# Small and large experts in turn, and part of the weight lows on GpSimd, in a two-block transformer kernel on one core

## The chip, the cores and the metric

The kernel runs on one NeuronCore of a Trainium2 chip. The time is device microseconds of one execution of the whole program. Lower is better.

## The reference

Two blocks are computed for 256 tokens of width 1024, everything in float32. The first has three attention branches and a SwiGLU feed-forward layer. The second has an HGRN2 layer with a feed-forward layer, then differential attention, and at the end a mixture of experts. Only the last part is touched by the change:

```
def moe_swiglu(h, w_router, w_gate, w_up, w_down):        # 256 tokens, D = 1024
    logits = (hf @ w_router).astype(jnp.float32)           # 8 experts
    top_val, top_idx = lax.top_k(logits, TOP_K)            # TOP_K = 2
    gates = jax.nn.softmax(top_val, axis=-1)
    ...
    return (jax.nn.silu(xb @ w_gate[e]) * (xb @ w_up[e])) @ w_down[e]   # D_FF_EXPERT = 3584
```

Each token goes to two of eight experts. An expert has three weight matrices of 1024 x 3584 (gate, up) and 3584 x 1024 (down), 44 MB in float32, and 352 MB are read for all eight.

## The kernel before

**Arithmetic.** A float32 product is made of three passes on TensorE in its faster float32 form: high part times high part, high times low and low times high (`mm3`, L425 to L427). So each weight has to be split. ScalarE makes the high part (`hi`, L1179) by a copy that rounds, and VectorE makes the low part, `lo = src - hi` (L1748), with both inputs in SBUF.

**Pieces.** The weights come through a ring of 2 MB slots, three and in the expert part four, by DMAs that SyncE issues in the order of the list `WL`. In the expert part one slot is two pieces of 128 x 2048. Each piece has one place out of four (`WHB0`, `WHB1`, `WHX0`, `WHX1` for the high parts, `WLB`/`WLX` for the low). ScalarE may make piece n only when TensorE has used piece n - 4 (`s_used`), VectorE when ScalarE has made the high part (`s_hi`), TensorE when VectorE has made the low (`s_lo`), and SyncE loads into a slot again when both its pieces have their low parts. An expert is 21 slots, so 42 pieces: 7 chunks of 512 hidden columns with 2 pieces each of gate, up and down. All eight make 336 pieces, in a list that is fixed when the program is built.

**Large and small experts.** Experts are taken in an order that the chip works out from the number of tokens of each (`order`, L2352 and on): `RANK[i]` says the expert of which rank is taken at turn i. Turn 0 is always expert 0, which the program counts as rank 0, and the others follow by size. Turns in `LIGHT` have room for 64 tokens, the others for 128. In a large turn TensorE makes three passes for each weight tile. In a small one the high and low part of 64 tokens stand side by side as one 128-column stationary operand, so that two passes do (L1007, L1008 for gate and up, L1053, L1054 for down): a piece is 12 matmuls of 512 columns in a large turn and 8 in a small one. A small turn also adds its halves up when the hidden values are turned (L1031) and has two short VectorE operations a chunk for it (L2412 and L2416), where a large turn has two longer ones (L2419 and L2426). Before, turns 1, 4 and 7 are small, and five are large. If an expert has more tokens than its turn has room for, a second pass over all experts (`pe_second` and its like) follows. It compares a count that the chip works out with a limit, and was not run in the execution shown.

**Order on the engines.** Each engine's program is written by hand. TensorE goes through the pieces one by one, gathers the next expert's tokens inside the last step of an expert (`gather`, L984 in small turns, L986 in large ones, the second half at the same place of each turn) and adds the one before to the result in between. ScalarE and VectorE have the pieces between the other work: ScalarE runs ahead of TensorE by up to four pieces in program order and VectorE by up to three (`split_to`). GpSimd has nothing to do in the expert part after the start but the roots of the last norm (L2574) and a quarter of its rows (L2596, L2598).

Of the kernel before, what the change touches and what calls it, by code (L numbers as in the profile page):

```python
# [8 lines left out]
F32 = mybir.dt.float32  # L9
# [3 lines left out]
ALU = mybir.AluOpType  # L13
# [7 lines left out]
NE = 8  # L21
# [7 lines left out]
LIM = 128  # L29
LIM_L = 64  # L30


RANK = (0, 5, 1, 2, 6, 3, 4, 7)
LIGHT = (1, 4, 7)


def steps_of(ex):
# [84 lines left out]
def build(nc, I, table, out):  # L122
    ctx = ExitStack()
    with ctx:
# [62 lines left out]
        def sem(name):  # L187
            return ctx.enter_context(nc.semaphore(name))
# [1 line left out]
        s_ring = [sem(f"s_ring{i}") for i in range(NSLOT + 1)]  # L190
        s_full = [sem(f"s_full{i}") for i in range(8)]
        s_out = [sem(f"s_out{i}") for i in range(8)]
        s_hi, s_lo, s_used = sem("s_hi"), sem("s_lo"), sem("s_used")
        s_colh, s_cols = sem("s_colh"), sem("s_cols")
        s_ms, s_rs, s_z, s_za = sem("s_ms"), sem("s_rs"), sem("s_z"), sem("s_za")
        s_ssq, s_ss1, s_sq = sem("s_ssq"), sem("s_ss1"), sem("s_sq")
# [84 lines left out]
        BEFORE = [max((j for j in range(i) if SLOT[j] == SLOT[i]), default=-1) for i in range(len(WL))]  # L281
# [3 lines left out]
        PIECES, PLACE, AFTER, LAST_OF = [], [], [], []  # L285
        FIRST = {}
        lay = {}
        for part_name, part_list, n_p in (("A", WL_A, 4), ("F1", WL_F1, 2), ("C", WL_C, 4), ("F2", WL_F2, 2), ("E", WL_E, 4), ("M", WL_M, 2)):
            FIRST[part_name] = len(PIECES)
            for item in part_list:  # L290
                step = -(-item[3] // n_p)
                for j in range(n_p):
                    k = len(PIECES)
# [11 lines left out]
                    PLACE.append(place)  # L305
                LAST_OF.append(len(PIECES) - 1)
        NP = len(PIECES)
        HIS, LOS = WHB + WHX, WLB + WLX

        def piece(k):  # L310

            i, t0, t1 = PIECES[k]
            n = WL[i][4]
            m = (t1 - t0) * n
            b, at = PLACE[k]
            return slot(i)[:, t0 * n:t1 * n], HIS[b][:, at:at + m], LOS[b][:, at:at + m]
# [90 lines left out]
        def pe_program(e):  # L407
            pe = Stream(e, s_pe)
# [6 lines left out]
            def next_piece(name, key):  # L415
                k = at[0]
                at[0] += 1
                i, t0, t1 = PIECES[k]
                assert WL[i][:2] == (name, key), (WL[i][:2], name, key)
                pe.wait_ge(s_lo, k + 1)  # L420
                _, hi, lo = piece(k)
                return hi.rearrange("p (t n) -> p t n", t=t1 - t0), lo.rearrange("p (t n) -> p t n", t=t1 - t0), (s_used, k + 1)

# [434 lines left out]
            for tt in range(2):  # L858
                for g in range(2):
# [9 lines left out]
                    for j in range(4):  # L869
# [3 lines left out]
                        if tt == 0:  # L873
                            t = e.matmul(o, STT[:, 0, h, :], v0, start=True, stop=True)
                        else:
                            e.matmul(o, STT[:, 2, h, :], v0, start=True, stop=False)
                            t = e.matmul(o, STT[:, 1, h, :], v1, start=False, stop=True)
# [859 lines left out]
        def dve_program(e):  # L1737
            v = Stream(e, s_dve)
            at = [0]

            def split_to(k):

                while at[0] <= min(k, NP - 1):
                    n = at[0]
                    at[0] += 1
                    src, hi, lo = piece(n)
                    v.wait_ge(s_hi, n + 1)
                    e.tensor_tensor(lo, src, hi.bitcast(F32), ALU.subtract).then_inc(s_lo, 1)  # L1748

            done = [0]  # L1750
# [198 lines left out]
            for i, w in enumerate((WFG, WRT)):  # L1949
                t = v.step(e.tensor_copy(W8[2 * i][:, :, :], w[:, :, :]))  # L1950
# [143 lines left out]
            t = v.step(e.tensor_tensor(LBM, L3[:, 0, :], L3[:, 1, :], ALU.max))  # L2094
            v.wait_ge(*t)
            t = v.step(e.tensor_tensor(LBM, LBM, L3[:, 2, :], ALU.max))
# [71 lines left out]
            for n in ("hg0", "hg1", "hv0", "hv1"):  # L2168
                for q in range(4):
# [3 lines left out]
                    if (n, q) in LEVEL_AT:  # L2173
                        i = LEVEL_AT[n, q]
# [177 lines left out]
            def order():  # L2352

                v.wait_ge(s_one, 2)
                t = v.step(e.memset(NCNT[:, 0:1], 999.0))
                v.wait_ge(*t)
                oth = NCNT.unsqueeze(1).to_broadcast([128, 8, 8])
                own = NCNT.unsqueeze(2).to_broadcast([128, 8, 8])
                v.step(e.tensor_tensor(C4[:, 0], oth, own, ALU.is_gt))
                t = v.step(e.tensor_tensor(C4[:, 1], oth, own, ALU.is_equal))  # L2360
                v.wait_ge(*t)
                t = v.step(e.tensor_tensor(C4[:, 1], C4[:, 1], tri, ALU.mult))
                v.wait_ge(*t)
                t = v.step(e.tensor_tensor(C4[:, 0], C4[:, 0], C4[:, 1], ALU.add))
                v.wait_ge(*t)
                t = v.step(e.tensor_reduce(RNK, C4[:, 0], AX.X, ALU.add))
                v.wait_ge(*t)
                t = v.step(e.tensor_scalar(CAPV, RNK, 4.5, float(LIM - LIM_L), ALU.is_lt, ALU.mult))
                eight = CT[:, C_IOTA:C_IOTA + 8]
                t2 = v.step(e.tensor_tensor(C4[:, 0], RNK.unsqueeze(1).to_broadcast([128, 8, 8]), eight.unsqueeze(2).to_broadcast([128, 8, 8]), ALU.is_equal))  # L2370
                v.wait_ge(*t)
                t = v.step(e.tensor_scalar(CAPV, CAPV, float(LIM_L), None, ALU.add))
                v.wait_ge(*t2)
                t2 = v.step(e.tensor_tensor(C4[:, 1], C4[:, 0], eight.unsqueeze(1).to_broadcast([128, 8, 8]), ALU.mult))
                v.wait_ge(*t2)
                t2 = v.step(e.tensor_reduce(MX8[:, 0, :], C4[:, 1], AX.X, ALU.add))
                v.wait_ge(*t2)
                e.tensor_copy(EID[:, :], MX8[0:1, 0, :]).then_inc(s_perm, 1)
                v.wait_ge(*t)
                v.wait_ge(s_rte, 2)  # L2380
                for src, dst in ((POS, POSR), (G, GR)):
                    if src is G:
                        v.wait_ge(s_gw, 2)
                    for tt in range(2):
                        t = v.step(e.tensor_tensor(Q4[:, tt], C4[:, 0], src[:, tt, :].unsqueeze(1).to_broadcast([128, 8, 8]), ALU.mult))
                    v.wait_ge(*t)
                    for tt in range(2):
                        t = e.tensor_reduce(dst[:, tt, :], Q4[:, tt], AX.X, ALU.add)
                    if src is G:
                        t.then_inc(s_gw, 1)  # L2390
                    else:
                        v.wait_ge(*v.step(t))
                t = v.step(e.tensor_tensor(MX8[:, 1, :], CNT0, CAPV, ALU.subtract))
                v.wait_ge(*t)
                t = v.step(e.tensor_reduce(MOST, MX8[:, 1, :], AX.X, ALU.max))
                v.wait_ge(*t)
                e.tensor_scalar(CNT[:, :], MOST[0:1, :], float(LIM), None, ALU.add).then_inc(s_most, 1)
# [171 lines left out]
        def pool_program(e):  # L2569
# [30 lines left out]
            def norm_vectors(k):  # L2600
                for j, name in enumerate(("ln_g_2", "ln_b_2")):
                    e.dma_start(BC[:, j, :], spread(I[name][k * D:k * D + D], D)).then_inc(s_ln, 16)
# [104 lines left out]
            p.wait_ge(s_hp, 11)  # L2707
            p.wait_ge(s_hd, 1)
            norm_vectors(3)
            for tt in range(2):  # L2710
                inverse_root(("ln3", tt))
            gain_rows(3, 1, 1)
# [4 lines left out]
        def sp_program(e):  # L2717
            q = Stream(e, s_pe)

            def source(i):  # L2720
                if WL[i][2] is not None:
                    return WL[i][2]
                kind, ex = WL[i][0].split()
                ex, at_ = int(ex), WL[i][1]
                w = I[f"moe_w_{kind}_2"]
                if ex and (kind, at_) == ("gate", (0, 0)):
                    q.wait_ge(s_perm, 1)
                    T["expert", ex] = e.value_load(EID[0:1, RANK[ex]:RANK[ex] + 1], min_val=0, max_val=NE - 1)
                w = w[bass.ds(T["expert", ex], 1)] if ex else w[0:1]
                if kind == "down":  # L2730
                    return w.rearrange("o (a p b) n -> p (o a) (b n)", p=128, b=2)[:, at_ // 2:at_ // 2 + 2, :]
                c0, k0 = at_
                return w.rearrange("o (t p) n -> p (o t) n", p=128)[:, k0:k0 + WL[i][3], c0:c0 + WL[i][4]]

            def load(i):
                t, n = WL[i][3:]
                if BEFORE[i] >= 0:
                    q.wait_ge(s_lo, LAST_OF[BEFORE[i]] + 1)
                elif SLOT[i] == NSLOT:
                    q.wait_ge(s_used, FIRST["E"])  # L2740
                    e.dma_start(CT2[:, :], table[:, C_LAST:C_END]).then_inc(s_tab2, 16)
                src = source(i)
                e.dma_start(slot(i)[:, 0:t * n].rearrange("p (t n) -> p t n", t=src.shape[1]), src).then_inc(s_ring[SLOT[i]], 16)

            load(0)
            e.dma_start(H[:, :, :], I["x"].rearrange("(a p) n -> p a n", p=128)).then_inc(s_x, 16)
            load(1)
            load(2)
            e.dma_start(LEVS, table[:, C_KEEP:C_LAST]).then_inc(s_lvt, 16)
            for i in range(NSLOT, len(WL)):  # L2750
                load(i)
            q.wait_ge(s_most, 1)
            q.wait_ge(s_lo, NP)
            n_most = e.value_load(CNT[0:1, 0:1], min_val=0, max_val=S + LIM)
            with e.If(n_most > LIM):
                sp_second(e)
            q.wait_ge(s_outd, 32)
# [148 lines left out]
```

## Time and profile before

| | us |
|---|---|
| runs (median, lowest, highest) | 2044.85, 2043.73, 2046.56 |
| profiled execution, its own time | 2045.65 |
| profiled execution, span of the trace | 2043.9 |

| engine | busy us | share |
|---|---|---|
| PE (TensorE matmul) | 1922.6 | 94% |
| DVE (VectorE) | 1507.5 | 74% |
| ACT (ScalarE) | 1211.3 | 59% |
| POOL (GpSimd) | 158.2 | 8% |

The span is that of the profiler from the first to the last instruction. The expert part takes the last half: its first piece is split at 1049.8 us and its last at 2007.6 us. In all rows "<-" in a name stands between what is written and what is read, and "<-" behind a wait stands ahead of what ended it. The rows further down are copied from the page and from views of the same trace.

### The profile page before, as it was taken

Reading aid. Unit: us, or ns where it says so; the run is one execution under the profiler, and the core shown is the slowest. Engines: PE = TensorE matmul, PEld = TensorE weight load, DVE = VectorE, ACT = ScalarE, POOL = GpSimd, SP = SyncE. Lnnn points to the kernel's source line nnn. Section 1 sums busy time; section 2 is a strip of 40 time slices with the busy share of each in tenths; the row PEclk is TensorE's granted clock in tenths of the full one; section 3 lists DMA queues with packets and bytes.
Section 4 is the critical chain, followed back from the end, with each engine's and each line's share of the span. In section 5 each row is a group of like instructions: output and inputs, shape, how many; then the busy total and the mean of one; then the engine's idle time right before and its main releaser. Section 6 shows DMA issues by size and latency. Waiting matters only on the chain.

```text
span 2043.9 us, 22687 instructions
## 1 busy us (share of the span) xinstructions
PE 1922.6 (94%) x9319; PEld 1583.1 (77%) x9319; DVE 1507.5 (74%) x1433; ACT 1211.3 (59%) x1229; POOL 158.2 (8%) x123
## 2 busy tenths in 40 slices
PE   5999999999998899989779999999999999999994
PEld 4778777888987688867557887888888788888873
DVE  4645456544689754476568889998988999898996
ACT  4554445433553444344336778876778887777883
POOL 1401010000133300031120000000000000000000
PEclk9999999999999899989778999999999999999997
DMA  8433334554432455344146999999999999999991
GB/s 275 150 136 127 124 124 166 205 185 169 161 124 83 168 205 203 127 162 165 42 169 231 376 359 404 409 397 352 351 364 366 411 408 387 351 359 363 373 409 75
DMA packets 154318, 511.64 MB, mean 250 GB/s; under 512 B 4334, under 2 KB 8672, under 8 KB 139872
## 3 DMA queue, kind: packets, MB, share of 16 engines
q1 hardware_dynamic: 151888, 502.91, 65.6%
q0 software_dynamic: 1424, 4.59, 0.8%
q10 hardware_dynamic: 896, 2.62, 0.3%
q8 instruction: 76, 1.25, 0.2%
q14 instruction: 34, 0.28, 0.0%
HBM read 509.05 MB, written 1.05 MB: 250 GB/s over the span
## 4 chain that ended last, share of the span: by engine, by line
PE 75%; DVE 14%; DMA 4%; ACT 3%; issue 2%; POOL 1%; DVEq 0%; SPq 0%; ACTq 0%; POOLq 0%
PE PS L425 21%; PE PS L427 21%; PE PS L426 21%; DVE WLB L1748 4%; DVE WLX L1748 4%; DMA ring<-in_moe_w_down 3%; PE PS L986 1%; PE PS L1053 1%; PE PS L1054 1%; DMA ring<-in_w_mem_kv 1%; PE PS L928 1%; PE PS L558 1%; ACT WHB L1179 1%; PE PS L1035 1%; DVE AR L2135 1%
## 5 line engine op out<-in xcount | busy, mean ns | idle before, releaser
L1748 DVE TENSOR_TENSOR WLB<-ring,WHB 128x2048 fp32r<-128x2048 f32 (+1 forms) x344 | 647.0, 1898 | 134.2 <-ACT WHB L1179 133.7
L1179 ACT ACTIVATE WHB<-ring 128x2048 fp32r<-128x2048 f32 (+1 forms) x344 | 534.5, 1562 | 347.7 <-PE PS L427 327.2
L1748 DVE TENSOR_TENSOR WLX<-ring,WHX 128x2048 fp32r<-128x2048 f32 (+1 forms) x216 | 468.4, 2190 | 56.7 <-ACT WHX L1179 56.5
L1179 ACT ACTIVATE WHX<-ring 128x2048 fp32r<-128x2048 f32 (+1 forms) x216 | 394.8, 1839 | 176.8 <-PE PS L427 156.8
L425 PE MATMUL PS<-WHB,XH 128*128 128x512 f32 (+1 forms) x640 | 258.9, 405 | 11.0 <-DVE XL L1799 6.8
L427 PE MATMUL PS<-WHB,XL 128*128 128x512 f32 (+1 forms) x640 | 252.0, 394 | 0.0
L426 PE MATMUL PS<-WLB,XH 128*128 128x512 f32 (+1 forms) x640 | 251.2, 393 | 0.0
L425 PEld LDWEIGHTS PS<-WHB,XH 128*128 128x128 f32 x640 | 123.5, 193 | 37.4 <-issue 11.5
L2574 POOL TENSOR_TENSOR SM<-SM,MH 128x8 f32<-128x8 f32 (+3 forms) x28 | 36.8, 1319 | 1468.7 <-DVE SM L1761 1468.7
L427 PEld LDWEIGHTS PS<-WHB,XL 128*128 128x128 f32 x640 | 122.9, 192 | 26.4
L426 PEld LDWEIGHTS PS<-WLB,XH 128*128 128x128 f32 x640 | 123.4, 193 | 23.9
L425 PE MATMUL PS<-WHB,EH 128*128 128x512 f32 x280 | 111.1, 397 | 0.0
L425 PE MATMUL PS<-WHX,EH 128*128 128x512 f32 x280 | 110.9, 396 | 0.0
L427 PE MATMUL PS<-WHB,EL 128*128 128x512 f32 x280 | 109.7, 392 | 0.0
L427 PE MATMUL PS<-WHX,EL 128*128 128x512 f32 x280 | 109.4, 391 | 0.0
L426 PE MATMUL PS<-WLB,EH 128*128 128x512 f32 x280 | 109.4, 391 | 0.0
L426 PE MATMUL PS<-WLX,EH 128*128 128x512 f32 x280 | 109.0, 389 | 0.0
L425 PE MATMUL PS<-WHX,XH 128*128 128x512 f32 (+1 forms) x240 | 92.0, 383 | 4.7 <-DVE WLX L1748 4.7
L425 PE MATMUL PS<-WHB,HTH 128*128 128x512 f32 x240 | 94.3, 393 | 0.0
L427 PE MATMUL PS<-WHB,HTL 128*128 128x512 f32 x240 | 93.5, 390 | 0.0
L426 PE MATMUL PS<-WLB,HTH 128*128 128x512 f32 x240 | 93.4, 389 | 0.0
L427 PE MATMUL PS<-WHX,XL 128*128 128x512 f32 (+1 forms) x240 | 91.1, 379 | 0.0
(398 smaller groups left out, 3472.6 us busy)
## 6 DMA issues: line engine op xcount, KB each, us to landing
ring<-in_moe_w_gate SPq DMA_DIRECT2D x56, 2048.0 KB, 9.9
ring<-in_moe_w_up SPq DMA_DIRECT2D x56, 2048.0 KB, 10.3
ring<-in_moe_w_down SPq DMA_DIRECT2D x56, 2048.0 KB, 10.3
ring<-in_w_in SPq DMA_DIRECT2D x13, 2048.0 KB, 8.1
ring<-in_hg_w_in SPq DMA_DIRECT2D x8, 2048.0 KB, 8.5
ring<-in_da_w_in SPq DMA_DIRECT2D x6, 2048.0 KB, 8.0
ring<-in_w_gate SPq DMA_DIRECT2D x5, 2048.0 KB, 8.6
ring<-in_w_up SPq DMA_DIRECT2D x5, 2048.0 KB, 7.8
```

Of the source, the lines that this page charges most:

```text
L425: e.matmul(o, xh, wh, start=start, stop=False)
L426: e.matmul(o, xh, wl, start=False, stop=False)
L427: return e.matmul(o, xl, wh, start=False, stop=stop)
L558: e.matmul(PS[2][:, a0:a1], q_[o:o + 64, j, 128 * qt:128 * qt + 128], k_[o:o + 64, j, 0:n], start=True, stop=False)
L928: e.matmul(PS[b][:, a0:a1], QD[o:o + 64, h, 128 * qt:128 * qt + 128], KD[o:o + 64, h, 0:n], start=True, stop=False)
L986: t = e.matmul(PS[b][:, 128 * j:128 * j + CAP], src[:, tt, 128 * d:128 * d + 128], PO[:, tt, :], start=(tt == 0), stop=(tt == 1))
L1035: t = e.transpose(PS[6][:, 128 * j:128 * j + 128], inner(HID[:, i, :], j), ident)
L1053: e.matmul(PS[4 + q][:, :], HTH[:, i, xs], hi[:, jj, cs], start=first, stop=False)
L1054: t = e.matmul(PS[4 + q][:, :], HTH[:, i, xs], lo[:, jj, cs], start=False, stop=end)
L1179: e.activation(hi, src, ACT.Copy).then_inc(s_hi, 1)
L1748: e.tensor_tensor(lo, src, hi.bitcast(F32), ALU.subtract).then_inc(s_lo, 1)
L2574: e.tensor_tensor(RR[name], RV[name], MH[:, 0:RR[name].shape[1]], ALU.pow).then_inc(s_rs, 1)
```

## The change

There are two edits. First, `RANK` and `LIGHT` make four turns large and four small, in turn: 0, 2, 4 and 6 are large and 1, 3, 5 and 7 small. The limit between large and small ranks follows (4.5 becomes 3.5). Second, from the ninth piece of the expert part on (`SHARED`), VectorE makes only the first 1536 of a piece's 2048 columns of the low part, and GpSimd makes the other 512, with the same operation and its own semaphore `s_lp`, for which TensorE and SyncE now also wait. GpSimd's 328 new instructions stand in its program between the loads of the last norm's vectors and the roots of that norm.

```
-RANK = (0, 5, 1, 2, 6, 3, 4, 7)
-LIGHT = (1, 4, 7)
+RANK = (0, 4, 1, 5, 2, 6, 3, 7)
+LIGHT = (1, 3, 5, 7)
+HEAVY = NE - len(LIGHT)
...
+        SHARED = FIRST["M"] + 8
+        OWN = 1536
...
                 pe.wait_ge(s_lo, k + 1)
+                if k >= SHARED:
+                    pe.wait_ge(s_lp, k - SHARED + 1)
...
                     src, hi, lo = piece(n)
                     v.wait_ge(s_hi, n + 1)
+                    if n >= SHARED:
+                        src, hi, lo = src[:, 0:OWN], hi[:, 0:OWN], lo[:, 0:OWN]
                     e.tensor_tensor(lo, src, hi.bitcast(F32), ALU.subtract).then_inc(s_lo, 1)
...
-                t = v.step(e.tensor_scalar(CAPV, RNK, 4.5, float(LIM - LIM_L), ALU.is_lt, ALU.mult))
+                t = v.step(e.tensor_scalar(CAPV, RNK, HEAVY - 0.5, float(LIM - LIM_L), ALU.is_lt, ALU.mult))
...
             norm_vectors(3)
+            for n in range(SHARED, NP):
+                src, hi, lo = piece(n)
+                p.wait_ge(s_hi, n + 1)
+                e.tensor_tensor(lo[:, OWN:], src[:, OWN:], hi[:, OWN:].bitcast(F32), ALU.subtract).then_inc(s_lp, 1)
             for tt in range(2):
                 inverse_root(("ln3", tt))
...
                 if BEFORE[i] >= 0:
                     q.wait_ge(s_lo, LAST_OF[BEFORE[i]] + 1)
+                    if LAST_OF[BEFORE[i]] >= SHARED:
+                        q.wait_ge(s_lp, LAST_OF[BEFORE[i]] - SHARED + 1)
...
             q.wait_ge(s_lo, NP)
+            q.wait_ge(s_lp, NP - SHARED)
```

TensorE at the start of turn 3, whose first gate piece lies in the place `WHX0`/`WLX0`; `EH` and `EL` are the high and low parts of the gathered tokens, `HID` the hidden values of the chunk before. Before, and then of the changed kernel:

```order
L427 MATMUL PS<-WHB1,HTL 128x512
L425 MATMUL PS<-WHX0,EH 128x512
L426 MATMUL PS<-WLX0,EH 128x512
L427 MATMUL PS<-WHX0,EL 128x512
L425 MATMUL PS<-WHX0,EH 128x512
L426 MATMUL PS<-WLX0,EH 128x512
L427 MATMUL PS<-WHX0,EL 128x512
L425 MATMUL PS<-WHX0,EH 128x512
```

```order
L433 MATMUL PS<-WHB1,HTL 128x512
L1013 MATMUL PS<-WHX0,EH 128x512
L1014 MATMUL PS<-WLX0,EH 128x512
L1013 MATMUL PS<-WHX0,EH 128x512
L1014 MATMUL PS<-WLX0,EH 128x512
L1013 MATMUL PS<-WHX0,EH 128x512
L1014 MATMUL PS<-WLX0,EH 128x512
L1013 MATMUL PS<-WHX0,EH 128x512
L1014 MATMUL PS<-WLX0,EH 128x512
```

The third pass of each weight tile is gone in this turn (the line numbers are higher by 6 to 16 through the edits themselves). Turns 4 to 7 change their kind as the new tables say.

VectorE in the second step of turn 3, before and then changed; L1748 is the low part of a piece (L1756 after the change), L2448 (L2456) adds a part of the expert before to the result:

```order
L1748 TENSOR_TENSOR WLB<-ring,WHB 128x2048
L1748 TENSOR_TENSOR WLX<-ring,WHX 128x2048 x2
L2426 TENSOR_TENSOR HID<-PS,HID 128x512 x2
L1748 TENSOR_TENSOR WLB<-ring,WHB 128x2048
L2448 TENSOR_TENSOR H<-H,PS 128x512
L1748 TENSOR_TENSOR WLB<-ring,WHB 128x2048
L1748 TENSOR_TENSOR WLX<-ring,WHX 128x2048 x2
L2419 TENSOR_TENSOR HTL<-PS,HTH 128x512
```

```order
L1756 TENSOR_TENSOR WLB<-ring,WHB 128x1536
L1756 TENSOR_TENSOR WLX<-ring,WHX 128x1536 x2
L2420 TENSOR_TENSOR SGT<-PS,SGT 128x256
L1756 TENSOR_TENSOR WLB<-ring,WHB 128x1536
L2424 TENSOR_TENSOR HTH<-SGT,HTH 128x4x64
L1756 TENSOR_TENSOR WLB<-ring,WHB 128x1536
L1756 TENSOR_TENSOR WLX<-ring,WHX 128x1536
L2456 TENSOR_TENSOR H<-H,PS 128x512
```

The pieces keep their places in the row and are shorter; the two operations on 512 columns of a large turn give way to two on 256.

GpSimd at the end of its program, before and then changed; the two DMAs are the vectors of the last norm, L2574 (later L2582) its roots:

```order
L2706 MEMSET HID 128x128
L2602 DMA BC<-in_ln_g_2 128x1024
L2602 DMA BC<-in_ln_b_2 128x1024
L2574 TENSOR_TENSOR SM<-SM,MH 128x1 x2
L2596 TENSOR_TENSOR H<-LZ,BC 128x512
L2598 TENSOR_TENSOR H<-H,BC 128x512
```

```order
L2714 MEMSET HID 128x128
L2610 DMA BC<-in_ln_g_2 128x1024
L2610 DMA BC<-in_ln_b_2 128x1024
L2721 TENSOR_TENSOR WLB0<-ring,WHB0 128x512
L2721 TENSOR_TENSOR WLB1<-ring,WHB1 128x512
L2721 TENSOR_TENSOR WLX0<-ring,WHX0 128x512
L2721 TENSOR_TENSOR WLX1<-ring,WHX1 128x512
```

The 328 new instructions follow one another, each behind the wait for its high part, and nothing else of GpSimd's stands between them.

## Rows read from the trace of the kernel before

**Rows 1.** The page, part 1: busy us, share of the span, instructions.
```profile
PE 1922.6 (94%) x9319; PEld 1583.1 (77%) x9319; DVE 1507.5 (74%) x1433; ACT 1211.3 (59%) x1229; POOL 158.2 (8%) x123
```

**Rows 2.** Busy time by stretch: PE, PEld, DVE, ACT, POOL, then PEclk, DMA share, GB/s.
```profile
1190.00:1297.00 107.00, 103.67 (x508) 84.06 (x506) 102.15 (x65) 90.53 (x72) 0.00 (x0) 1.00 0.99 386
...
1417.00:1541.00 124.00, 124.00 (x579) 103.55 (x578) 108.17 (x67) 89.44 (x61) 0.00 (x0) 1.00 0.94 355
1541.00:1648.00 107.00, 104.03 (x512) 84.66 (x511) 102.63 (x65) 91.19 (x73) 0.00 (x0) 1.00 0.99 389
```

**Rows 3.** Chain of waits, longest parts: start us, us; second gathers, ahead of turns 1 to 7.
```profile
1190.94 1.71 PE PS L984 x16
...
1296.30 1.74 PE PS L986 x16
...
1417.77 1.74 PE PS L986 x16
...
1541.94 1.71 PE PS L984 x16
...
1646.79 1.74 PE PS L986 x16
...
1768.26 1.74 PE PS L986 x16
...
1892.43 1.71 PE PS L984 x16
```

**Rows 4.** Instructions in order of time, PE: the last matmul on weights.
```profile
2017.70 0.39 PE L1054 MATMUL PS<-WLX,HTH 128*128 128x512 f32 x1
```

**Rows 5.** Waits in 1190 to 1297 us (a small turn): total us, times, longest.
```profile
PEld PS L1007 <- DVE WLB L1748: 2.9, 5, 1.1
...
DVE WLB L1748 <- ACT WHB L1179: 2.7, 2, 2.3
```

**Rows 6.** Waits in 1417 to 1541 us (a large turn).
```profile
ACT WHB L1179 <- PE PS L427: 18.1, 20, 2.2
```

**Rows 7.** Instructions in order of time, DVE, small turn: start us, us for all, count.
```profile
1233.62 4.49 DVE L1748 TENSOR_TENSOR WLX<-ring,WHX 128x2048 fp32r<-128x2048 f32 x2
```

**Rows 8.** The same view near the start, pieces of half the size.
```profile
79.91 2.36 DVE L1748 TENSOR_TENSOR WLB<-ring,WHB 128x1024 fp32r<-128x1024 f32 x2
...
85.71 1.21 DVE L1748 TENSOR_TENSOR WLB<-ring,WHB 128x1024 fp32r<-128x1024 f32 x1
```

**Rows 9.** The same view, POOL, while DVE has nothing under way.
```profile
704.48 1.30 POOL L2598 TENSOR_TENSOR H<-H,BC 128x512 f32<-128x512 f32 x1
```

**Rows 10.** The same view, POOL and DVE from 603 to 611 us.
```profile
604.29 4.47 POOL L2664 TENSOR_TENSOR BC<-BC,NG 128x512 f32<-128x512 f32 x2
```
```profile
602.25 3.18 DVE L2135 TENSOR_TENSOR AR<-AR 128x1024 f32<-128x1024 f32 x1
605.35 4.50 DVE L1748 TENSOR_TENSOR WLB<-ring,WHB 128x1024 fp32r<-128x1024 f32 x2
```

**Rows 11.** The same view, DVE: one instruction beside POOL's, and without.
```profile
896.92 1.25 DVE L2047 SCALAR_TENSOR_TENSOR SM<-SM 128x1 f32<-128x1 f32 x1
```
```profile
1047.53 0.16 DVE L2047 SCALAR_TENSOR_TENSOR SM<-SM 128x1 f32<-128x1 f32 x1 [0.66 <-POOL SM L2574]
```

**Rows 12.** The same view, POOL and DVE from 260.7 to 261.8 us.
```profile
260.70 1.28 POOL L2635 TENSOR_TENSOR AR<-AR 128x512 f32<-128x512 f32 x1 [65.03 <-DVE AR L1897]
```
```profile
260.54 1.89 DVE L1897 TENSOR_TENSOR AR<-PS,AR 128x512 f32<-128x512 f32 x3
```

**Rows 13.** DVE by groups, 1190 to 1297 us, then 1417 to 1541 us: busy us, mean ns.
```profile
L1748 DVE TENSOR_TENSOR WLX<-ring,WHX 128x2048 fp32r<-128x2048 f32 x22 | 49.9, 2285 | 1.2 <-ACT WHX L1179 1.2
...
L2416 DVE TENSOR_TENSOR HTH<-SGT,HTH 128x256 fp32r<-128x256 f32 x5 | 2.1, 418 | 0.0
```
```profile
L2419 DVE TENSOR_TENSOR HTL<-PS,HTH 128x512 fp32r<-128x512 f32 x7 | 4.8, 689 | 5.5 <-ACT HTH L1638 5.5
```

**Rows 14.** Busy time by stretch, 20 us inside a small turn.
```profile
1620.00:1640.00 20.00, 19.91 (x106) 16.68 (x104) 19.78 (x16) 17.43 (x15) 0.00 (x0) 1.00 1.02 413
```

More of the change, by code:

```diff
@@ L192, in build @@
         s_out = [sem(f"s_out{i}") for i in range(8)]
-        s_hi, s_lo, s_used = sem("s_hi"), sem("s_lo"), sem("s_used")
+        s_hi, s_lo, s_lp, s_used = sem("s_hi"), sem("s_lo"), sem("s_lp"), sem("s_used")
         s_colh, s_cols = sem("s_colh"), sem("s_cols")
```

## The prediction

> **What bounds the kernel now.** I read the page first: TensorE is busy for 94% of the span and VectorE for 74%, GpSimd for 8% [rows 1]. That share is a mean over stages, so the second view is busy time by stretch, one stretch for each expert turn. A large turn (1417 to 1541 us) has TensorE busy for all of its 124 us and VectorE for 108.17. A small one (1190 to 1297) has VectorE at 102.15 of 107 and the DMA engines at 0.99 [rows 2]. Third come the waits. In the small turn TensorE's weight loads wait for VectorE's low parts, and VectorE waits only 2.7 us for ScalarE [rows 5]; in the large one ScalarE waits for TensorE to free a place [rows 6]. So large turns are TensorE's, and small turns VectorE's, with the DMA close behind.
>
> The length of a turn is best read on TensorE, from the second gather of one turn to that of the next, 42 pieces apart [rows 3]: small turns take 1296.30 - 1190.94 = 105.4 and 1646.79 - 1541.94 = 104.9 us; a large turn behind a small one 1417.77 - 1296.30 = 121.5 and again 121.5; a large one behind a large one 124.2 and again 124.2. Behind the last gather come 48 pieces (six of turn 6, and turn 7), which end with the last matmul on weights at 2018.1 [rows 4]: 125.7 us, which is 48/42 of 105.2 and 5.5 for the drain. From 1190.94 to 2018.1 are 827.2 us. Before the first gather there are 36 pieces of turn 0, which is large in both kernels.
>
> **Edit one, the order of the turns.** The kinds from turn 1 on were S L L S L L S and become S L S L S L S. One large turn becomes small, and each large one then stands behind a small one. By the rows: 3 x (105.2 + 121.5) + 125.7 = 805.8 us, 21.4 less. A small turn does not go below its 105 even if VectorE is helped: an expert is 168 instructions less on TensorE but the same 44.04 MB (21 slots of 2.097 MB), and at the 413 GB/s of the busiest rows [rows 14] these take 106.6 us. So the DMA is what is late next, and the first edit alone, or both if GpSimd cost nothing, is worth about -21 us.
>
> **Edit two, who makes the low part.** VectorE's piece: two of 2048 columns in a row take 4.49 us, one 2.285 [rows 7, 13], so each further one adds 2.21. Of 1024 columns it is 2.36 for two and 1.21 for one [rows 8], so 1.15. For 1536 I take the middle, 1.68. GpSimd's 512 columns take 1.30 us alone [rows 9], well under the 2.5 to 3.0 that a piece lasts in a turn, so it would be hidden if the two engines ran side by side.
>
> They don't. At 604 us GpSimd had two operations of just this size (512 columns, both inputs in SBUF) while VectorE made two low parts of 1024 columns: GpSimd's two took 4.47 us and not 2.6, VectorE's two 4.50 and not 2.36 [rows 10]. GpSimd's first could not run before VectorE's L2135 ended at 605.43; from there to 609.85, the end of VectorE's second, both had two to do, and 4.42 us is the sum of both. The engines took turns, each waiting for the whole of the other's instruction. Per pair it is 4.47 / 2 = 2.23 us, of which 1.15 are VectorE's, so 512 columns of GpSimd's hold VectorE up for 1.08. Even an operation on one column waits so: 1.25 us beside GpSimd's, 0.16 without [rows 11]. Where VectorE reads one operand from PSUM, neither is slowed: three of 512 columns in 1.89 us and GpSimd's at 1.28 [rows 12].
>
> The Trainium skill says why, in "SBUF — State Buffer", section "Who interferes with whom": a VectorE instruction with two SBUF inputs gets its second one through the read interface that it shares with GpSimd, and it and a GpSimd instruction that reads SBUF exclude each other for a whole instruction. By that rule this change moves work from an engine to a port that the same engine needs; by the plain reading of the GpSimd row alone it would be free.
>
> So the two engines together need 1.68 + 1.08 = 2.76 us a piece, where VectorE alone needed 2.21. The sum over the engines' timelines:
>
> - A small turn: 42 x 2.76 = 115.9. L2416 also has both inputs in SBUF: seven of 0.42, less the overlap of 0.07 between neighbours, are 2.4. The other VectorE work of a small turn reads PSUM (L2412, L2448, ZL, POT). What a turn has besides pieces is 105.2 - 42 x 2.21 = 12.4 us. Most of it can lie beside GpSimd's piece, since GpSimd's turn comes behind each VectorE piece and a short PSUM operation fits into 1.08. I leave 1.2 exposed, one in six of the operations. That is 119.5 us against 105.2.
> - A large turn: TensorE needs 124.2 in the steady state and 121.5 behind a small one. VectorE now needs 115.9 and its 14 operations L2419 and L2426 of 0.69, the combines, and waits for ScalarE of 5.5 us before L2419 [rows 13]; hidden in the same way they leave some 5. So VectorE needs about 121 of what TensorE needs 121.5. I take 121.5, no change, but the slack of 124 - 108 that let VectorE get ahead for the next small turn is gone.
> - Before the first gather: 36 pieces of a large turn, 28 of them shared, at 2.76 less than TensorE's own 124.2 / 42 = 2.96. I take +1.
> - The last 48 pieces: 119.5 x 48 / 42 + 5.5 = 142.1, against 125.7.
>
> Together 1 + 3 x (119.5 + 121.5) + 142.1 = 866.1, against 827.2: +38.9 us, made of -21.4 from the order and +60 from the taking of turns. The rest costs nothing: TensorE's and SyncE's second waits are for an engine that isn't behind VectorE, because GpSimd's row is not held up by other work; a slot is then freed with VectorE's part as now, and the loads, at 0.94 to 0.99 of the DMA's time before [rows 2], get more time. Behind GpSimd's 328 instructions stand only the roots of the last norm, which wait for the end anyway. On the profiled time of 2045.65 that gives 2084.5; its distance to the median of the runs (-0.8) leaves 2083.7.
>
> The bounds of what the trace doesn't show, the overlap: if nothing but pieces and L2416 is exposed, a small and a large turn take 2 x 115.9 + 2.4 = 234.2 together (TensorE can be late in the large one and catch up in the small), the end 118.3 x 48 / 42 + 5.5 = 140.7, and the sum is 1 + 702.6 + 140.7 - 827.2 = +17. If nothing is hidden, a small turn is 115.9 + 12.4 = 128.3, a large one 115.9 + 15 = 131, the end 152: 2 + 778 + 152 - 827 = +105. With no exclusion at all it is -21. I am nearer to the lower end since the alternation in [rows 10] leaves the 1.08 us slot behind every piece.
>
> **Rivals.**
> 1. The two engines do not exclude each other here, or hardly: faster. It would hold if GpSimd fell into VectorE's PSUM operations and idle time always, or if the lock hung on the operands used at 604 us. Place: small turns. Price: 2045.65 - 21.4 - 0.8, 2023 us. For it: in a small turn VectorE has 12.4 us of such time and GpSimd is free to run ahead of it. Against it: GpSimd needs 42 x 1.08 = 45 us, nearly four times that. The point from which it decides: the order gives 21.4 us, the small turns and the end have 174 pieces, so a piece in them may cost 2.51 + 0.12 = 2.63 us with all around it, and the pieces alone take 2.76 by [rows 8 to 10]. The Trainium skill has a table in "SBUF — State Buffer", section "A bandwidth-pool intuition that's wrong (but worth ruling out)", that gives HBM about 358 GB/s a core; by it a small turn would need 123 us, and no order of turns could gain. The measured 413 decides here.
> 2. Excluded, but all else hidden: the +17 above, 2062 us, and down to 2050 if GpSimd holds VectorE up for 1.04 us and not 1.08 (328 x 0.04 = 13). For it: GpSimd has no other work to be queued behind. Against it: ScalarE can be only four pieces ahead of TensorE, so GpSimd often has nothing to do just when VectorE turns to a PSUM operation.
> 3. Excluded, and the engines' hand-offs get in each other's way: VectorE's late L2419 holds TensorE up in large turns too, since the slack that hid it is gone. Up to +105, 2150 us. For it: four places are little room.
> 4. The change doesn't do what it says, because the fifth expert in size has over 64 tokens and the second pass runs. The routing worked out from the reference on its inputs gives 127, 28, 62, 85, 35, 37, 41 and 97 tokens. Expert 0 is large anyway, then 97, 85 and 62; the first small one has 41. So it doesn't run. It would read 352 MB again, at 413 GB/s 853 us more.
>
> **How the numbers follow.** My forecast, 2062 to 2112 us, has 0.70; rival 1 0.10, rival 2 0.11, rival 3 (2112 to 2150) 0.08, rival 4 0.01. The range of 8 in 10 is 2052 to 2112: it leaves out rival 1 and the top. What a measurement of this kernel can tell from no change is 0.2%, 4 us. Faster by more: rival 1 and a little, 0.11. Within it: 0.04, from the lower end of rival 2. Slower: 0.85.
>
> **What would show it.** In the profile after, GpSimd's pieces should last 2 to 2.8 us and not 1.3 where VectorE is at work, and VectorE's 1536-column pieces up to 2.8, not 1.75, so that VectorE's busy time in the expert part grows although it has a quarter less to do. Small turns should be 117 to 123 us apart and large ones 120 to 125. TensorE should wait for VectorE's low parts in small turns for over 10 us. It is wrong if VectorE's pieces have a mean under 1.9 us or small turns stay near 105. The granted clock should stay at 1.00 in the turns; if it falls in the small ones, where TensorE now idles more, they last longer than said.

## The result and the profile after

The changed kernel takes 2080.1 us (median of 4 runs, 2078.24 to 2082.75); the kernel before, on the same chip, 2044.62. The ratio is 1.0173, 95% interval 1.0156 to 1.0191: slower by 35.5 us. The forecast was 2084, in a range from 2052 to 2112. The profiled execution has a span of 2080.9 us.

The second gathers of the turns in the chain of waits (start us, us), which answer to [rows 3]:

```profile
1192.22 1.71 PE PS L990 x16
...
1433.32 1.71 PE PS L990 x16
...
1553.12 1.74 PE PS L992 x16
...
1674.63 1.71 PE PS L990 x16
...
1795.54 1.73 PE PS L992 x16
...
1917.07 1.71 PE PS L990 x16
```

The one missing in this view, ahead of turn 2, starts at 1310.23 in the order of time, where all the others start 0.16 us earlier than here, so it counts as 1310.4. So the small turns 1, 3 and 5 take 118.2, 119.8 and 120.9 us (before: 105.4 and 104.9), the large turns 2, 4 and 6 take 122.9, 121.5 and 121.5. The last matmul on weights ends at 2055.1, 138.0 us after the last gather, against 125.7.

Busy time by stretch, for turns 1 to 4, with the columns of [rows 2]:

```profile
1192.00:1310.00 118.00, 105.85 (x494) 83.00 (x494) 112.95 (x63) 90.74 (x71) 103.76 (x42) 0.99 0.96 360
1310.00:1433.00 123.00, 122.17 (x580) 101.88 (x579) 119.91 (x73) 90.25 (x64) 90.28 (x43) 1.00 0.99 373
1433.00:1553.00 120.00, 107.47 (x497) 84.20 (x496) 114.96 (x65) 91.15 (x71) 101.05 (x42) 0.97 0.96 360
1553.00:1674.50 121.50, 121.50 (x580) 101.95 (x579) 116.62 (x71) 90.00 (x64) 94.72 (x43) 1.00 0.98 372
```

VectorE (third pair) has a quarter less to subtract and is busy for 113 to 120 us a turn instead of 102 to 108. GpSimd is busy for 90 to 104 us with work that needs 42 x 1.3 = 55 alone. The DMA engines move 360 GB/s in the small turns instead of 386 to 389, at a share of 0.96 and not 0.99. They are not the limit there any more: in turn 1 the chain of waits has no load in it, VectorE's pieces are 78% of it, and none of ScalarE's waits there is for a load.

The groups of the two engines from 1110 to 1950 us (busy us, mean ns, idle before), to be held against [rows 13] and [rows 9]:

```profile
L1756 DVE TENSOR_TENSOR WLB<-ring,WHB 128x1536 fp32r<-128x1536 f32 x146 | 359.5, 2476 | 15.9 <-ACT WHB L1185 15.5
...
L2721 POOL TENSOR_TENSOR WLX<-ring,WHX 128x512 fp32r<-128x512 f32 x146 | 353.2, 2429 | 76.7 <-ACT WHX L1185 76.4
...
L2424 DVE TENSOR_TENSOR HTH<-SGT,HTH 128x256 fp32r<-128x256 f32 x21 | 21.0, 999 | 4.4 <-ACT HTH L1641 4.4
```

A VectorE piece of 1536 columns lasts 2.48 us on average, more than one of 2048 did (2.285). In order of time, inside turn 1, first VectorE and then GpSimd:

```profile
1229.55 1.51 DVE L2424 TENSOR_TENSOR HTH<-SGT,HTH 128x256 fp32r<-128x256 f32 x1
1230.97 2.84 DVE L1756 TENSOR_TENSOR WLX<-ring,WHX 128x1536 fp32r<-128x1536 f32 x1
1233.73 2.83 DVE L1756 TENSOR_TENSOR WLB<-ring,WHB 128x1536 fp32r<-128x1536 f32 x1
1236.49 0.68 DVE L2456 TENSOR_TENSOR H<-H,PS 128x512 f32<-128x512 f32 x1
1237.09 2.23 DVE L1756 TENSOR_TENSOR WLB<-ring,WHB 128x1536 fp32r<-128x1536 f32 x1
```
```profile
1227.97 2.80 POOL L2721 TENSOR_TENSOR WLX<-ring,WHX 128x512 fp32r<-128x512 f32 x1
1230.73 4.22 POOL L2721 TENSOR_TENSOR WLB<-ring,WHB 128x512 fp32r<-128x512 f32 x2
1234.91 2.79 POOL L2721 TENSOR_TENSOR WLX<-ring,WHX 128x512 fp32r<-128x512 f32 x1
```

The two steps from 1230.97 to 1233.73 to 1236.49 are 2.76 us each, the sum that the prediction had: 1.68 of VectorE's and 1.08 of GpSimd's. At 1236.49 VectorE turns to an operation that reads PSUM; it is not lengthened (0.68), GpSimd's turn lies beside it, and the piece behind it has only 2.23 instead of 2.84. That is the hiding that the sum counted on. The 256-column L2424, with both inputs in SBUF, has 1.51 instead of 0.42.

Who waits in turn 1 (total us, times, longest), for [rows 5]:

```profile
PEld PS L1013 <- DVE WLX L1756: 9.0, 7, 2.5
...
PEld PS L1013 <- DVE WLB L1756: 4.9, 7, 1.1
```

TensorE's weight loads wait 13.9 us for VectorE in these two rows. They hardly wait for GpSimd's part; in the groups from 1110 to 1950 us:

```profile
L1013 PE MATMUL PS<-WHX,EH 128*128 128x512 f32 x184 | 76.4, 415 | 16.9 <-DVE WLX L1756 16.2 <-POOL WLX L2721 0.7
L1013 PE MATMUL PS<-WHB,EH 128*128 128x512 f32 x184 | 76.0, 413 | 9.1 <-DVE WLB L1756 7.5 <-POOL WLB L2721 1.3
```

### The profile page after: what moved, and what is told of

Its sections match the earlier page's. It is cut to its first block, busy times and chain, and to the rows that moved or that the text cites. A ratio compares the mean times of both kernels' runs of the same rounds, so it can differ in the third digit from the quotient of the medians.

```text
span 2080.9 us, 23288 instructions
## 1 busy us (share of the span) xinstructions
PE 1915.5 (92%) x9235; PEld 1564.0 (75%) x9235; DVE 1581.4 (76%) x1431; ACT 1216.3 (58%) x1243; POOL 934.0 (45%) x451
## 4 chain that ended last, share of the span: by engine, by line
PE 65%; DVE 28%; issue 3%; ACT 3%; DMA 1%; POOL 1%; DVEq 0%; ACTq 0%; POOLq 0%
PE PS L431 18%; PE PS L433 18%; PE PS L432 18%; DVE WLB L1756 10%; DVE WLX L1756 10%; PE PS L1059 1%; PE PS L1060 1%; DVE HTH L2424 1%; PE PS L934 1%; DMA ring<-in_w_mem_kv 1%; PE PS L564 1%; DVE AR L2143 1%; PE PS L992 1%; PE PS L845 1%; PE PS L990 1%
## 5 line engine op out<-in xcount | busy, mean ns | idle before, releaser
L1756 DVE TENSOR_TENSOR WLB<-ring,WHB 128x1536 fp32r<-128x1536 f32 (+2 forms) x344 | 680.0, 1992 | 134.1 <-ACT WHB L1185 133.6
L1756 DVE TENSOR_TENSOR WLX<-ring,WHX 128x1536 fp32r<-128x1536 f32 (+2 forms) x216 | 495.5, 2317 | 54.6 <-ACT WHX L1185 54.5
L2721 POOL TENSOR_TENSOR WLX<-ring,WHX 128x512 fp32r<-128x512 f32 x164 | 401.0, 2455 | 85.4 <-ACT WHX L1185 85.0
L2721 POOL TENSOR_TENSOR WLB<-ring,WHB 128x512 fp32r<-128x512 f32 x164 | 379.5, 2322 | 113.1 <-ACT WHB L1185 112.3
L2582 POOL TENSOR_TENSOR SM<-SM,MH 128x8 f32<-128x8 f32 (+3 forms) x28 | 36.2, 1300 | 532.7 <-DVE SM L1769 532.7
L431 PEld LDWEIGHTS PS<-WHB,XH 128*128 128x128 f32 x640 | 122.8, 192 | 38.9 <-issue 11.4
L1013 PE MATMUL PS<-WHX,EH 128*128 128x512 f32 x224 | 92.9, 415 | 18.2 <-DVE WLX L1756 17.5
L1013 PE MATMUL PS<-WHB,EH 128*128 128x512 f32 x224 | 92.4, 412 | 11.7 <-DVE WLB L1756 10.1
L432 PE MATMUL PS<-WLX,XH 128*128 128x512 f32 (+1 forms) x240 | 91.3, 380 | 0.0
L431 PE MATMUL PS<-WHX,EH 128*128 128x512 f32 x224 | 89.3, 399 | 0.6 <-DVE WLX L1756 0.6
L1014 PE MATMUL PS<-WLX,EH 128*128 128x512 f32 x224 | 89.1, 398 | 0.0
L431 PE MATMUL PS<-WHB,EH 128*128 128x512 f32 x224 | 88.6, 396 | 0.2 <-DVE WLB L1756 0.2
L1014 PE MATMUL PS<-WLB,EH 128*128 128x512 f32 x224 | 88.2, 394 | 0.0
```

Of the source, the lines that this page charges most:

```text
L431: e.matmul(o, xh, wh, start=start, stop=False)
L432: e.matmul(o, xh, wl, start=False, stop=False)
L1013: e.matmul(PS[b][:, :], EH[:, kt, :], wh, start=(kt == 0), stop=False)
L1014: t = e.matmul(PS[b][:, :], EH[:, kt, :], wl, start=False, stop=(kt == 7))
L2582: e.tensor_tensor(RR[name], RV[name], MH[:, 0:RR[name].shape[1]], ALU.pow).then_inc(s_rs, 1)
L2721: e.tensor_tensor(lo[:, OWN:], src[:, OWN:], hi[:, OWN:].bitcast(F32), ALU.subtract).then_inc(s_lp, 1)
```

## The experiments

Times are medians. Ratios are to the kernel before on the same chip. "Small" and "large" give the distances of the second gathers, as above, and "end" the time from the last gather to the last matmul on weights.

**Each edit alone.** The order alone:

```
 RANK = (0, 4, 1, 5, 2, 6, 3, 7); LIGHT = (1, 3, 5, 7); HEAVY = NE - len(LIGHT)
 e.tensor_scalar(CAPV, RNK, HEAVY - 0.5, ...)        # nothing of SHARED, OWN, s_lp
```

> The first edit alone: four large and four small turns in turn, VectorE makes the whole of each low part. Theory (the order gains, GpSimd's share loses): 21.4 us less than before, about 2023 us; small turns 105, large ones 121.5 us apart. Rival (the order itself costs, for example because small turns now always stand beside large ones and the DMA is late): at or over 2045 us. A third outcome, under 2010, would say that a small turn can go below the 105 us that the DMA seemed to set.

Measured: 2025.96 us, ratio 0.9893 (0.9876 to 0.9910), 20 us less than 2045.78. The chain of waits:

```profile
1191.76 1.71 PE PS L985 x16
...
1297.66 1.74 PE PS L987 x16
...
1419.16 1.71 PE PS L985 x16
...
1525.83 1.74 PE PS L987 x16
```

Small 105.9, large 121.5, small 106.7; turn 5, not shown, has 105.6. These are the lengths of before in another order, the small ones about 1 us longer. GpSimd's share alone:

```
 # the changed kernel, with
-RANK = (0, 4, 1, 5, 2, 6, 3, 7)
-LIGHT = (1, 3, 5, 7)
+RANK = (0, 5, 1, 2, 6, 3, 4, 7)
+LIGHT = (1, 4, 7)
```

> The second edit alone: the order of before (large, small, large, large, small, large, large, small), GpSimd makes the last quarter of the low parts. Theory: small turns 119.5, large ones behind a small one 122, behind a large one 124 (TensorE still sets those), so 1 + 2 x 119.5 + 2 x (122 + 124.2) + 142 = 874 us against 827: +47, about 2091 us. Rival (the share costs only together with the new order): near 2045. Rival (hand-offs between three engines hold up large turns too): each of the five large turns grows by 5 to 10 us, 2110 to 2140 us.

Measured: 2086.42 us, ratio 1.0188 (1.0169 to 1.0207), 41 us more. Small 119.3 and 118.2, large behind a small one 121.5 and 122.9, large behind a large one 124.2 twice, end 138.0. The large turns hardly grew, which sets the second rival aside; each small one grew by 13 to 14. The 5 us that are missing to the 2091 expected are mostly the end, expected at 142. The two edits do not quite add up: -20 and +41 would make +21, and both together cost +35.5, because the share costs about 14 us for every small turn and the order adds a small turn. That is also what the sum of the prediction does.

**What the two engines exclude each other through.** GpSimd writes zeros and reads nothing; all waits and VectorE's 1536 columns stay:

```
-e.tensor_tensor(lo[:, OWN:], src[:, OWN:], hi[:, OWN:].bitcast(F32), ALU.subtract).then_inc(s_lp, 1)
+e.memset(lo[:, OWN:].bitcast(F32), 0.0).then_inc(s_lp, 1)
```

> The changed kernel, but GpSimd only writes zeros to its 512 columns and reads nothing; its waits, its semaphore, TensorE's and SyncE's waits for it and VectorE's 1536 columns stay. The low parts of a quarter of each weight piece are left out of the result by this. Theory (VectorE and GpSimd exclude each other through what both read): VectorE's pieces fall to 1.75 us, small turns to about 105 (the DMA), total 2023 us, as with the order alone. Rival (the extra waits and semaphores, or the order in which three engines meet, cost the time): 2070 to 2085 us, VectorE's pieces as short as 1.75 and the waits long. Rival (any SBUF access of GpSimd's excludes VectorE, writes too): VectorE's pieces 1.75 plus the length of the writing, small turns 110 or more, 2035 to 2060.

Measured: 2025.45 us, ratio 0.9891 (0.9872 to 0.9911), the time of the order alone. The groups from 1110 to 1950 us:

```profile
L1756 DVE TENSOR_TENSOR WLX<-ring,WHX 128x1536 fp32r<-128x1536 f32 x156 | 272.5, 1754 | 49.7 <-ACT WHX L1185 48.6
...
L2721 POOL MEMSET WLX<- 128x512 f32 x155 | 81.7, 527 | 333.9 <-ACT WHX L1185 333.9
```

All 328 pieces of VectorE's have 1.75 us. So the 55 us between this kernel and the changed one are neither the semaphores nor the waits of TensorE and SyncE; they come with what GpSimd reads, or with the shorter instruction (0.53 us and not 1.27), which the next run tells apart. The 0.53 us of writing are not waited for. The busy time in turn 1 of this kernel shows what is late next:

```profile
1190.00:1297.00 107.00, 102.96 (x505) 85.78 (x503) 82.92 (x66) 90.76 (x73) 22.42 (x43) 0.98 0.99 390
```

VectorE is down to 82.9 us of 107, and the turn is still 105.7 us long, with the DMA engines at 0.99. TensorE is nearly as busy, 102.96 us, so the shares don't say which of the two is the limit. The chain of waits does. Between 1222.8 and 1289.1 us it has no piece of TensorE's; 40 of these 66 us are three loads:

```profile
1231.43 11.62 DMA ring<-in_moe_w_up
...
1249.67 13.80 DMA ring<-in_moe_w_gate
...
1269.19 14.58 DMA ring<-in_moe_w_down
```

In the kernel before, VectorE's pieces stood there from 1221 to 1272 us, and only one load behind them. So the 105 us of a small turn are VectorE's and, within 1 us, those of the loads: at 390 to 413 GB/s the 44 MB of an expert take 107 to 113 us, no less than the turn (the loads run ahead a little in the large ones). Relief of VectorE alone did not shorten it.

Then a GpSimd operation with one input in SBUF:

```
+e.tensor_scalar(lo[:, OWN:], src[:, OWN:], 0.0, None, ALU.mult).then_inc(s_lp, 1)
```

> As the run with zeros, but GpSimd reads one input: it multiplies its 512 columns of the weights by zero (the low parts of a quarter of each piece are left out of the result). Theory: a GpSimd instruction that reads one input also excludes VectorE, for its own length; it should be some 0.5 us for 512 columns (one of 2048 took 1.92 us before), so VectorE needs 1.68 + 0.5 = 2.2 us a piece, as before the change: VectorE's pieces up to 2.3, GpSimd's up to 2.3, small turns 105 to 109, total 2023 to 2035. Rival (only GpSimd's two-input reads exclude): VectorE's pieces all 1.75, GpSimd's all at their length alone, 2023.

Measured, one execution: 2025.23 us. The total fits, and so does VectorE's longest piece, but the reason given did not:

```profile
L2721 POOL TENSOR_SCALAR WLX<-ring 128x512 fp32r<-128x512 f32 x156 | 358.0, 2302 | 83.5 <-ACT WHX L1185 83.2
...
L1756 DVE TENSOR_TENSOR WLX<-ring,WHX 128x1536 fp32r<-128x1536 f32 x156 | 286.3, 1845 | 39.1 <-ACT WHX L1185 38.3
```

```profile
1228.31 1.75 DVE L1756 TENSOR_TENSOR WLX<-ring,WHX 128x1536 fp32r<-128x1536 f32 x1
1229.98 2.16 DVE L1756 TENSOR_TENSOR WLB<-ring,WHB 128x1536 fp32r<-128x1536 f32 x1
```

GpSimd's instruction has at the least 1.48 us, three times what was expected, and 2.3 on average, so it does wait for VectorE. But it holds VectorE up by 2.16 - 1.75 = 0.41 us at the most, and VectorE's mean is only 1.84. The hold is not the length of the instruction. Nor is a long or late instruction on GpSimd what costs the 55 us: these are longer than the subtractions' 1.27 us alone, and the total is that of the order alone. What is left as the cause is GpSimd's reading of two inputs while VectorE has two. The Trainium skill ("SBUF — State Buffer", section "Summary: rules for kernel authors") says that of a VectorE instruction with two SBUF inputs and a GpSimd one that reads SBUF the second to issue is fully blocked until the first has finished. With two inputs that nearly came out (1.08 of 1.27 to 1.30 us), with one input the measurement differs.

**The size of the share.**

```
-        OWN = 1536
+        OWN = 1792        # and, in the second run, 1024
```

> The changed kernel with GpSimd's share halved: 1792 columns on VectorE, 256 on GpSimd. Theory (each piece takes VectorE's columns at 1.15 us per 1024 plus a hold by GpSimd in proportion to its columns): 1.95 + 0.5 = 2.45 us a piece, small turns 42 x 2.45 + 3.6 = 106.5, so 2027 to 2034 us, a little over the run with the order alone (2026). Rival (what GpSimd holds is mostly a fixed cost of an instruction): 1.95 + 1.0 = 2.95 us a piece, slower than the changed kernel, over 2095.

Measured: 2037.37 us, ratio 0.9953 (0.9936 to 0.9971); its profiled execution, 2031.0, is at the low end of its runs. In that one, small turns take 108.2, 108.5 and 108.2 us.

> The changed kernel with GpSimd's share doubled: 1024 columns each. Theory (the sum law): VectorE 1.15 + GpSimd 2.2 = 3.35 us a piece in all turns, small and large turns both near 145 us, 2245 to 2275 us. Rival (fixed cost of an instruction): 1.15 + 1.1 = 2.25 us a piece, no slower than before the share, about 2026.

Measured, one execution: 2258.34 us. Small turns 142.2, 143.9 and 144.0, large 142.4, 142.1 and 145.7. VectorE in turn 1 of the two runs, 1792 columns first:

```profile
1236.21 2.55 DVE L1756 TENSOR_TENSOR WLB<-ring,WHB 128x1792 fp32r<-128x1792 f32 x1
1239.28 2.01 DVE L1756 TENSOR_TENSOR WLB<-ring,WHB 128x1792 fp32r<-128x1792 f32 x1
```
```profile
1239.11 3.41 DVE L1756 TENSOR_TENSOR WLB<-ring,WHB 128x1024 fp32r<-128x1024 f32 x1
```

With 256 columns on GpSimd the hold is 2.55 - 2.01 = 0.54 us; with 1024 it is 3.41 less the 1.21 of a piece of 1024 columns alone [rows 8], 2.2. The hold goes with the columns, not with the instruction: per column GpSimd costs VectorE 2.1 ns and takes 1.12 ns of work from it. So none of the shares pays: 2026 without, 2037, 2080 and 2258 us with an eighth, a quarter and a half, and by the price per column a smaller one could not either. At an eighth I was some 3 us too low in the median; the small turns took 108.2 us and not 106.5.

**Where the price is paid.** The share in large turns alone:

```
+        BY_POOL = [n for n in range(SHARED, NP) if int(WL[PIECES[n][0]][0].split()[1]) not in LIGHT]
...
-                    if n >= SHARED:                 # VectorE; GpSimd's loop and the waits for s_lp likewise
+                    if n in BY_POOL:
```

> The changed kernel with GpSimd's share in large turns alone; in small turns VectorE makes the whole low part. Theory (large turns have room on VectorE, small ones none, so the price is paid in the small turns): large turns stay at 121.5 to 123, small turns lose some 2 us since VectorE enters them without its lead, 2028 to 2040 us. Rival (hand-offs in large turns cost as much): large turns 125 or more, over 2045.

Measured: 2028.45 us, ratio 0.9918 (0.9888 to 0.9948), not to be told from the order alone (0.9893, 0.9876 to 0.9910). Turn 2, which is large, in the busy times:

```profile
1294.00:1416.00 122.00, 121.38 (x576) 101.22 (x575) 117.23 (x70) 90.61 (x64) 80.15 (x38) 1.00 0.99 386
```

VectorE is at 117 of 122 us there, and the three large turns take 122.7 us each by the gathers, 1.2 more than with the order alone; the small ones take 105.5, 106.0 and 105.5. Over the six turns that is 2.4 us more than with the order alone. So nearly all of the price is in the small turns, as the sum had it, and 160 subtractions on GpSimd are free where VectorE has room. They buy nothing there either.

**A faster version.** The order alone, with one more small turn:

```
-RANK = (0, 4, 1, 5, 2, 6, 3, 7)
-LIGHT = (1, 3, 5, 7)
+RANK = (0, 3, 4, 1, 5, 6, 2, 7)
+LIGHT = (1, 2, 4, 5, 7)
```

> The order alone, taken further: large turns 0, 3 and 6, small turns 1, 2, 4, 5 and 7 (on these inputs the fourth expert in size has 62 tokens), no share for GpSimd. Theory: one more large turn becomes a small one, 121.5 to 106: 2010 us. Rival (a small turn behind a small one finds VectorE without a lead and the DMA at its limit, so it takes 110 or more): 2015 to 2020.

Measured: 2011.8 us, ratio 0.9820 (0.9794 to 0.9846), the fastest kernel of this study. Its gathers:

```profile
1190.88 1.71 PE PS L985 x16
...
1298.07 1.71 PE PS L985 x16
...
1404.95 1.74 PE PS L987 x16
...
1526.43 1.71 PE PS L985 x16
```

A small turn behind a small one has 106.9 us here, and the other such one 106.8, so the rival is refuted. The two behind a large one have 107.2 and 109.3 in this execution, the slowest of the four (2016.35 us). The kernel is safe on inputs like these, where the fourth expert in size has 62 tokens for its 64 places; with 65 the second pass over all weights would run.

## Why the prediction was right

- **What bounds which turn** was read rightly: the large turns stayed at TensorE's pace with the share on (121.5 to 122.9 us) and the small ones, with the end, took nearly all of its price.
- **The order, -21.4 us.** Measured alone: -20 us. The statement that the DMA keeps a small turn at 105 us is borne out by the run in which VectorE needs only 83 us of it and the loads stand in the chain of waits in its place.
- **2.76 us a piece.** Shown by the steps in the trace after, and by the run that reads nothing (1.75 us a piece). The step that carried the prediction was a single stretch of the trace before [rows 10] in which both engines had two inputs in SBUF. GpSimd's time alone [rows 9] would have led to -21 us. The reading has a small slip: the 4.47 us that were halved begin 1.14 us before L2135 ended, while GpSimd's first was waiting for it. From the 4.42 us of the same paragraph the hold is 1.06 and the piece 2.74; the steps measured after have 2.76.
- **What is hidden.** Taken were 119.5 us for a small turn and 121.5 for a large one. Measured 119.6 and 122.0 on average. That GpSimd's slot is partly hidden behind VectorE's PSUM operations is seen in the trace. The 1.2 us left exposed ("one in six") came from no row, though, and single small turns have from 118.2 to 120.9 us, so that the mean came out within 0.1 us is partly luck.
- **The end, +16.4 us,** is the term that was mis-sized: 138.0 us and not 142.1. I scaled it from whole small turns. In the last pieces VectorE is hardly held up any more: GpSimd has made its part of the pieces that ScalarE had ready and then sits idle for 4.64 us until the next. VectorE, and then GpSimd:

```profile
2041.46 1.75 DVE L1756 TENSOR_TENSOR WLB<-ring,WHB 128x1536 fp32r<-128x1536 f32 x1
2043.28 1.76 DVE L1756 TENSOR_TENSOR WLX<-ring,WHX 128x1536 fp32r<-128x1536 f32 x1
```
```profile
2043.32 5.60 POOL L2721 TENSOR_TENSOR WLX<-ring,WHX 128x512 fp32r<-128x512 f32 x2 [4.64 <-ACT WHX L1185]
```

That, the start (+1.3 for 1), the small turns (+0.4 in all) and the large ones (+1.4 in all) make the difference between the +38.9 of the sum and the 37.0 us between 2018.1 and 2055.1, where the last matmul on weights ends. Two pieces without their hold are 2.2 of the end's 4.1 us; the rest was not taken apart.
- **The granted clock** was foreseen at 1.00 in the turns. It is 0.97 in turn 3 and 0.99 in turn 1 of the changed kernel, where TensorE waits more. Turn 3 is 1.6 us longer than turn 1; the runs don't separate the clock's part in it. In the run with zeros the first two small turns had 0.98 and took 105.7 and 107.0 us; with the order alone they had 1.00 and took 105.9 and 106.7.
- **The rivals.** No exclusion: refuted by the pieces' length. Excluded, but all else hidden (2062 us or less): a small and a large turn together would take 234.2 us; they take 241.1, 241.3 and 242.4, and the total is 18 us above it. Large turns held up by hand-offs: refuted by the share alone and by the share in large turns alone. The second pass did not run.

## What to carry to other kernels

Before an idle engine is given part of a busy one's work, look in the trace for a stretch in which both have run the same kind of instruction together, and compare the lengths there with those alone; one such stretch was worth more than both engines' busy shares. For subtractions with both inputs in SBUF, GpSimd and VectorE did not work as two engines: each column moved to GpSimd cost VectorE nearly twice what it saved. And when several stages have different limits, it is cheaper to change how many stages of each kind there are than to relieve the engine of one of them, whose next limit (here the DMA, within 1 us) may be as near.

## What the runs showed of the hardware

- A GpSimd instruction with two inputs in SBUF holds up a VectorE instruction with two by 0.54, 1.08 and 2.2 us for 256, 512 and 1024 columns. A GpSimd memset of 512 columns does not hold it up at all (328 of 328 pieces at their own length).
- With one input, GpSimd's multiplication of 512 columns takes 1.48 us at the least, longer than the subtraction with two (1.27), and yet holds VectorE up by 0.41 at the most.
- The hold does not depend on VectorE's size: 256 columns of L2424 have 0.42 us alone and 1.51 beside GpSimd.
